# A decoder layer on one core: the projection groups of g set ahead of those of i and av

## The reference

```python
h = rmsnorm(x, norm_pre_mix)
proj = einsum('bsd,de->bse', h, w_in)
hq, hf, hi, hg, aq, ak, av, iq, ik, iw = split(proj)
y_a = hgrn2_mixer(hq, hf, hi, hg, lb, hgrn_gnorm)   # gated linear recurrence, 4 heads of 128
y_b = dsa_mixer(aq, ak, av, iq, ik, iw, rel_bias)   # top-128 keys by the indexer, then attention
x = x + rmsnorm(concat(y_a, y_b) @ w_o, norm_post_mix)
x = x + rmsnorm(SwiGLU(rmsnorm(x, norm_pre_ffn)), norm_post_ffn)
```

## Time and profile before

| | us |
|---|---|
| median of 3 timed runs | 757.66 (757.44 to 758.81) |
| the profiled execution | 756.03 |
| its span, first to last instruction | 754.3 |
| PE busy in the span | 709.1 |
| DVE busy | 411.0 |
| ACT busy | 268.2 |
| POOL busy | 121.3 |

### The profile page before, as it was taken

One profiled execution on the slowest core, in us unless ns is written; L12 is line 12 of the kernel. 1 busy time (PEld: TensorE's weight loads), 2 busy tenths in 40 slices (PEclk: granted clock), 3 DMA queues, 4 the chain that ended last, 5 costly groups with the idle time before them and its releaser, 6 DMA issues.

```text
span 754.3 us, 9087 instructions
## 1 busy us (share of the span) xinstructions
PE 709.1 (94%) x3744; PEld 606.4 (80%) x3744; DVE 411.0 (54%) x582; ACT 268.2 (36%) x374; POOL 121.3 (16%) x129
## 2 busy tenths in 40 slices
PE   3889999888999997899999999999999999999996
PEld 2867779888989787898889888888888888888885
DVE  3574899788894997744566234334433433122125
ACT  6455544313442826633344213222332222122112
POOL 4400225353130305720210000000000000000001
PEclk9999999999999997999999999999999999999999
DMA  8513122111143120034222232233233313322302
GB/s 271 190 35 95 47 75 94 57 56 56 56 123 102 54 96 19 1 113 143 81 84 73 96 111 85 84 111 112 71 97 112 112 60 108 112 94 73 112 0 111
DMA packets 50088, 67.57 MB, mean 90 GB/s; under 512 B 4096, under 2 KB 43008, under 8 KB 50048
## 3 DMA queue, kind: packets, MB, share of 16 engines
q1 hardware_dynamic: 46512, 60.59, 25.0%
q0 software_dynamic: 2096, 6.30, 2.4%
q10 hardware_dynamic: 1440, 0.11, 0.1%
HBM read 64.87 MB, written 3.69 MB: 91 GB/s over the span
## 4 chain that ended last, share of the span: by engine, by line
PE 75%; DVE 17%; ACT 4%; issue 2%; DMA 1%; POOL 1%; DVEq 0%; SPq 0%; ACTq 0%
PE PS L969 64%; PE PS L1036 4%; DVE w_lo L671 3%; DVE A L713 2%; DVE top L712 2%; PE PS L1130 2%; DVE A L798 1%; DVE A L797 1%; DVE QK L780 1%; PE PS L1061 1%; DMA A<-in_x_dram 1%; DVE A L821 1%; PE PS L1008 1%; PE PS L1049 1%; DVE A L882 1%
## 5 line engine op out<-in xcount | busy, mean ns | idle before, releaser
L969 PE MATMUL PS<-hT_lo,w_hi 128*128 128x512 f32 (+2 forms) x584 | 220.2, 377 | 7.9 <-DVE w_lo L671 6.1
L671 DVE TENSOR_TENSOR w_lo<-raw,w_hi 128x2048 fp32r<-128x2048 f32 x51 | 125.2, 2455 | 172.7 <-ACT w_hi L480 172.5
L969 PE MATMUL PS<-hT_hi,w_lo 128*128 128x512 f32 (+2 forms) x584 | 219.2, 375 | 0.0
L969 PE MATMUL PS<-hT_hi,w_hi 128*128 128x512 f32 (+2 forms) x584 | 219.0, 375 | 0.0
L480 ACT ACTIVATE w_hi<-raw 128x2048 fp32r<-128x2048 f32 x51 | 97.6, 1913 | 205.9 <-PE PS L969 205.8
L969 PEld LDWEIGHTS PS<-hT_lo,w_hi 128*128 128x128 f32 (+1 forms) x584 | 111.4, 191 | 28.2 <-DVE w_lo L671 4.8
L969 PEld LDWEIGHTS PS<-hT_hi,w_hi 128*128 128x128 f32 (+1 forms) x584 | 111.4, 191 | 19.8
L969 PEld LDWEIGHTS PS<-hT_hi,w_lo 128*128 128x128 f32 (+1 forms) x584 | 111.3, 191 | 18.8
L969 PE MATMUL PS<-w_hi,ff 128*128 128x512 f32 x352 | 109.1, 391 | 0.0
L382 POOL TENSOR_SCALAR ms<-ss 128x1 f32<-128x1 f32 (+1 forms) x17 | 7.7, 454 | 451.7 <-ACT raw L655 358.0
L969 PEld LDWEIGHTS PS<-w_hi,ff 128*128 128x128 f32 x352 | 66.1, 188 | 14.0
(11 more groups left out here) (156 smaller groups left out, 841.2 us busy)
## 6 DMA issues: line engine op xcount, KB each, us to landing
raw<-in_w_in_dram SPq DMA_DIRECT2D x16, 1024.0 KB, 5.5
raw<-in_w_gate_dram SPq DMA_DIRECT2D x11, 1024.0 KB, 5.3
raw<-in_w_up_dram SPq DMA_DIRECT2D x11, 1024.0 KB, 5.3
raw<-in_w_down_dram SPq DMA_DIRECT2D x11, 1024.0 KB, 4.9
raw<-in_w_o_dram SPq DMA_DIRECT2D x4, 1024.0 KB, 5.0
A<-in_x_dram SPq DMA_DIRECT2D x4, 512.0 KB, 7.9
A<-in_x_dram POOLq DMA_DIRECT2D x4, 512.0 KB, 5.3
out_dram<-A SPq DMA_DIRECT2D x8, 256.0 KB, 2.1
```

The costliest lines, as they stand in the source:

```text
L671: dve.tensor_tensor(lo, raw_view(j), hi.bitcast(F32), ALU.subtract).then_inc(s_lo, 1)
L969: o = pe.matmul(out, lhs[a], rhs[b], start=(first and n == 0), stop=(last and n == 2))
```

## The change

The order of the kinds in the list is changed from f, q, i, av, g, aq, ak to f, q, g, i, av, aq, ak, and the number of the first level is counted from the first group of g instead of i. Nothing else is edited.

```diff
     chunks = [("iq", 0), ("iq", 1), ("ikw", 0)]
-    chunks += [(s, c) for s in ("f", "q", "i", "av", "g", "aq", "ak") for c in range(2)]
+    chunks += [(s, c) for s in ("f", "q", "g", "i", "av", "aq", "ak") for c in range(2)]
...
-    G_L0 = first_group["i"] + 1
+    G_L0 = first_group["g"] + 1
```

## The result

The changed kernel takes 761.16 us (median of 5, 759.4 to 761.99), the kernel before 757.66 on the same chip: ratio 1.0044 with a 95% interval of 1.0028 to 1.006, so 3.3 us slower (2.1 to 4.5). Forecast were 760.7 us and +3.0 us. One of all timed runs here, 810.39 us in a_fill05 at a mean granted clock of 0.84, was in a slower state; the ratio leaves it out, the median doesn't.

What follows compares the result with a forecast made beforehand. The prediction took VectorE, alternating with TensorE, to bound groups 13 to 19 and TensorE alone group 20 to the end of 28. 0.61 + 1.17 + 1.2 = +3.0 us on 757.66 gave 760.7 us, range 758.0 to 762.6.

Steps and rivals of the forecast that it cites:

- The regimes: Groups 13 to 19: path through VectorE, TensorE waiting; group 20 to the end of 28: TensorE itself, without a gap.
- silu_mul(13): On VectorE ahead of level 0's operands, where VectorE is never idle: level 0 starts 0.61 us later.
- silu_mul(14) to (16): On VectorE between a level's operands and its merges, hidden because TensorE paces the last merge: 0.
- Matmul form: Groups 21 to 24 on TensorE become 48-matmul projections, 0.29 us longer each, without idle time: +1.17 us.
- Table loads: ACT's sigmoid/exp switches up to the attention, 7 loads instead of 5, 1.28 us each, in idle time: 0.
- Rival 3: ACT's table loads do reach the path at level 2: +0.6 us on the sum, 761.3 us; chance 0.07.
- The clock at level 0: TensorE's longer idle time brings the lower clock to level 0's matmuls: +1.2 us (0 to 1.63).
- The wait ahead of level 0: TensorE's idle time before level 0's matmuls grows to 3.0 us instead of 1.66.
- Rival 2: Not slower: low clock behind the wait at 259.93 goes, 1.6 us back, level 0 keeps the clock: 757.9 us; chance 0.14.
- The sum: Whole kernel: 0.61 + 1.17 + 1.2 = +3.0 us, 760.7 us, 0.4% slower.

Runs made afterwards that it cites:

- a_fill05: The changed kernel with matmuls whose results are overwritten unread put into TensorE's idle time ahead of level 0 (8) and level 5 (7) alone: 758.62 us, 1.0006.
- a_fill: The changed kernel with 42 matmuls, results overwritten unread, in TensorE's idle time ahead of levels 0, 1, 3, 5 and groups 5, 29: 753.73 us, 0.9958 of the kernel before.
- b_fill: The kernel before with 38 unread matmuls in TensorE's idle time at the same places as a_fill, 4 instead of 8 ahead of level 0: 752.95 us, 0.9944.
- b_late: The kernel before with four more VectorE multiplications of 512 columns in group 13, where silu_mul(13) stands after the change: 763.89 us, 1.0089.
- a_defer_fill5: The changed kernel with silu_mul(13) put behind level 0's operands and 7 unread matmuls ahead of level 5: 759.08 us, 1.0027 of the kernel before.
- a_fill0: The changed kernel with 8 unread matmuls in TensorE's idle time ahead of level 0 alone: 759.49 us, 1.0034 of the kernel before.
- a_defer: The changed kernel with silu_mul(13) put behind the operands of level 0 on VectorE, no added matmuls: 761.1 us, 1.0052 of the kernel before.
- b_fill_late: The kernel before with b_late's four VectorE multiplications and unread matmuls in TensorE's idle time, 13 of them ahead of level 0: 756.59 us, 0.9981.

## Why the prediction was right

- **The regimes** held. Groups 13 to 19 run through VectorE: what the g groups save on TensorE shows as idle time (0.72 instead of 0.42 us ahead of level 2, with every later level interval unchanged).
- **silu_mul(13), +0.61:** measured 0.61 in the profiles and 0.60 with fillers. Deferred, it is gone to 0.01 us.
- **silu_mul(14) to (16), 0:** level 0 to 1 takes 12.13 us in a_fill and 12.17 in b_fill, level 1 to 2 10.03 and 10.02, level 2 to 3 12.47 in both, with and without silu_mul between operands and merge. In a_fill the last merge of level 0 starts 3.87 us after the level, as before.
- **Matmul form, +1.17:** measured 1.18, and undone by the form alone.
- **Table loads, 0:** seven loads as counted, none before the attention's first exp, and their removal moves nothing. Rival 3 is out. The Trainium skill, "ScalarE: Activation LUTs", section "What ACT_TABLE_LOAD costs", adds a drain of 1.38 us to the load for every switch of set. This case's traces don't show one: in the profile after, too, exp starts 1.3 us after the load begins.

```profile
125.82 1.28 ACT L546 ACT_TABLE_LOAD   x1
127.12 1.91 ACT L546 ACTIVATE A<-A 128x2048 f32<-128x2048 f32 x1
```

- **The clock at level 0, +1.2 (0 to 1.63):** right in kind, the size too small. It was 2.81 us in the profile of after, 2.21 in b_late, 1.63 in a_defer_fill5; by the times 2.3. This is the term that was mis-sized, and its bound of 1.63 was wrong: it was read from levels 1 and 3, where the clock was low for 3.4 us and only a part of the matmuls ran slow (5.47 us for 32). It took for granted, without a row for it, that a low stretch at level 0 would be no longer. It was 6.8 us long, with 6.0 of them in the level, and 6.69 - 3.84 = 2.85 us is what it cost. Even that is no bound: a level wholly at half the clock would cost its 3.84 us once more (an estimate). Why the stretch was twice as long there, after a wait of 2.88 us, and not at levels 1 and 3, after 2.81 and 2.89, is not known.
- **The wait ahead of level 0:** forecast 3.0 us, measured 2.88.
- **Rival 2's price was wrong.** A low stretch behind the wait at 259.93 was put at 1.6 us. In the profile after it did not come, and the interval from group 29 to the attention is 28.37 us against 28.35. VectorE's split for group 31 paces it: TensorE at full clock waits 1.44 us at 280.79, a wait that the profile of before, with the low stretch, doesn't have. So that rival could not have given a result of "not slower" in this way.
- **The sum** came within 0.5 us of the median (760.7 and 761.16). Part of it is luck. In the profile the terms are 0.61 + 1.18 + 2.81 = 4.6 us, while the times show 3.3 (2.1 to 4.5). The level at which the clock falls differs from execution to execution (a_fill0, a_defer and b_late lost it at level 5, before and after did not), so a fall gained at level 0 may in part be one that is not had elsewhere. That is argued, not shown: how often each level falls in the timed runs was not measured.

What stays open is what decides between keeping and losing the clock after 1.8 to 2.4 us of idle time. Ahead of the levels every wait of up to 1.81 us (b_fill_late, level 0) kept it and every one of 2.58 us and more lost it. The wait of 2.40 us ahead of level 5 kept it in before and after and lost it in a_fill0 and b_late; the wait of 1.82 us ahead of group 29 lost it in before and kept it in after.

## What to carry to other kernels

When two engines take turns on the path, moving work between stages costs where the path runs through the engine that gets it, and brings nothing where it leaves an engine that already waits; ask for each moved piece which engine's timeline is free of gaps at the old and at the new place. Idle time of TensorE has a price beyond its length, since the matmuls behind it may run at half the clock: price it at up to the full length of what follows, and not by what the nearest fall in the trace cost. Where TensorE's work behind the wait is on the path, fill the wait with matmuls that nobody reads, fewer than fit into it. Here that was done for waits of 1.66 to 2.9 us, and it gave 4.2 us to the kernel before (0.9944) and 6.5 us to the changed one, more than the reordering lost.

## What was not expected of the hardware

- Useless matmuls make the kernel faster: 38 of them take 0.6% off the kernel before, 42 take 0.9% off the changed one. In the row of a_fill eight take 1.97 us.
- Waits of the same length, in the same places of nearly the same kernels, kept the clock in one profile and lost it in another: 2.07 to 2.08 us (ahead of group 5: held in before, fell in after), 2.40 us (level 5), 1.82 us (group 29). At level 0 it held after 2.28 and fell after 2.23.
- A fall of the clock has no fixed price: where another engine paces the stretch it cost nothing that shows (group 29 to the attention, 28.35 us with it and 28.37 without), at level 5 1.63 us, and at level 0 2.81.
- Without the clock, intervals of some 10 us repeat to 0.02 us from kernel to kernel, while timed medians of the same kernel differ by over 1 us (756.92 to 758.24 for the kernel before, on different chips). A term of 0.6 us can be read from the intervals and not from the times.
